# A third of the down projection's ring with its stationary chunks at other distances, modulo 512 bytes, from the moving half

## The reference

```python
up = causal_dwconv(jnp.einsum('bsd,df->bsf', h, ffn_w_up[l]), ffn_conv_w[l]) + ffn_conv_b[l]
gate, val = jnp.split(up, 2, axis=-1)
ff = jnp.einsum('bsf,fd->bsd', jax.nn.silu(gate) * val, ffn_w_down[l])
x = x + rms_norm(ff, norm_ffn_post[l])
```

## Time and profile before

| | us |
|---|---|
| median of 3 runs | 950.27 |
| lowest and highest run | 950.18, 951.21 |
| the profiled execution's span | 948.2 |
| TensorE busy | 938.9 (99%) |
| weight loads busy | 777.9 (82%) |
| DVE, ACT, POOL busy | 654.7, 433.5, 189.4 |
| down projection, first to last matmul | 732.9 to 942.6 |

### The profile page before, as it was taken

One profiled execution on the slowest core, in us unless ns is written; L12 is line 12 of the kernel. 1 busy time (PEld: TensorE's weight loads), 2 busy tenths in 40 slices (PEclk: granted clock), 3 DMA queues, 4 the chain that ended last, 5 costly groups with the idle time before them and its releaser, 6 DMA issues.

```text
span 948.2 us, 11487 instructions
## 1 busy us (share of the span) xinstructions
PE 938.9 (99%) x4419; PEld 777.9 (82%) x4419; DVE 654.7 (69%) x710; ACT 433.5 (46%) x648; POOL 189.4 (20%) x182
## 2 busy tenths in 40 slices
PE   8999999999999999999999999999999999999997
PEld 7988887887888888888888888888888888888886
DVE  6645795766655899777877787778776653535668
ACT  5524444444433555445443444444444454335353
POOL 3301000000111424242223333443431100000021
PEclk9999999999999999999999999999999999999999
DMA  6999971005322236486343446554647775677455
GB/s 225 269 328 231 209 145 45 23 23 178 134 89 89 90 97 206 142 184 183 115 141 100 145 112 133 112 143 105 140 91 208 201 235 214 228 267 264 163 171 200
DMA packets 114248, 151.16 MB, mean 159 GB/s; under 512 B 6289, under 2 KB 66193, under 8 KB 114193
## 3 DMA queue, kind: packets, MB, share of 16 engines
q1 hardware_dynamic: 100737, 118.63, 38.5%
q0 software_dynamic: 13456, 31.79, 16.8%
HBM read 113.17 MB, written 60.29 MB: 183 GB/s over the span
## 4 chain that ended last, share of the span: by engine, by line
PE 97%; DVE 1%; DMA 0%; ACT 0%; POOL 0%; issue 0%; DVEq 0%; POOLq 0%; SPq 0%; ACTq 0%
PE ps L1616 30%; PE ps L1618 30%; PE ps L1617 30%; PE ps L1626 1%; PE ps L1751 1%; PE ps L1774 1%; PE ps L1752 1%; PE ps L1760 1%; PE ps L1778 1%; DMA xin<-in_x 0%; DVE hlo L1138 0%; PE ps L1789 0%; DVE ps L1155 0%; PE ps L1664 0%; DVE x2b L1427 0%
## 5 line engine op out<-in xcount | busy, mean ns | idle before, releaser
L1616 PE MATMUL ps<-hhi,whi 128*128 128x512 f32 (+1 forms) x240 | 91.1, 379 | 0.5 <-DVE hlo L1138 0.5
L1618 PE MATMUL ps<-hhi,wlo 128*128 128x512 f32 (+1 forms) x240 | 88.5, 369 | 0.0
L1617 PE MATMUL ps<-hlo,whi 128*128 128x512 f32 (+1 forms) x240 | 88.5, 369 | 0.0
L686 POOL TENSOR_TENSOR w_sums<-wraw 128x1024 f32<-128x1024 f32 x20 | 48.4, 2421 | 185.8 <-DVE w2lo L1373 63.0
L648 POOL TENSOR_SCALAR meansq<-sumsq 128x1 f32<-128x1 f32 x28 | 10.0, 357 | 373.4 <-ACT yg L1042 170.8
L1616 PEld LDWEIGHTS ps<-hhi,whi 128*128 128x128 f32 x240 | 45.3, 189 | 8.0 <-DVE hlo L1138 0.7
L1001 ACT ACTIVATE yg<-ps,par_b 128x1024 f32<-128x1024 f32 x21 | 25.3, 1207 | 57.9 <-DVE ps L1499 57.9
L1618 PEld LDWEIGHTS ps<-hhi,wlo 128*128 128x128 f32 x240 | 45.2, 189 | 7.7
L1617 PEld LDWEIGHTS ps<-hlo,whi 128*128 128x128 f32 x240 | 45.3, 189 | 7.4 <-issue 0.5
L1447 DVE SCALAR_TENSOR_TENSOR yg<-ps,par_a,yg 128x1023 f32<-128x1023 f32 x22 | 28.2, 1282 | 26.9 <-ACT yg L1001 26.9
L1616 PE MATMUL ps<-h2hi,whi 128*128 128x512 f32 x116 | 45.4, 391 | 0.2 <-DVE wraw L1148 0.2
(11 more groups left out here) (261 smaller groups left out, 2709.1 us busy)
## 6 DMA issues: line engine op xcount, KB each, us to landing
wraw<-in_ffn_w_up SPq DMA_DIRECT2D x42, 512.0 KB, 5.2
s_dram<-in_ffn_w_down POOLq DMA_DIRECT2D x6, 2816.0 KB, 28.1
wraw<-r_dram SPq DMA_DIRECT2D x44, 256.0 KB, 3.7
wraw<-s_dram SPq DMA_DIRECT2D x44, 256.0 KB, 4.9
r_dram<-cst SPq DMA_DIRECT2D x33, 256.0 KB, 2.8
wraw<-act_dram SPq DMA_DIRECT2D x33, 256.0 KB, 3.6
wraw<-in_ffn_w_down SPq DMA_DIRECT2D x33, 256.0 KB, 4.6
wraw<-in_w_in SPq DMA_DIRECT2D x14, 512.0 KB, 10.2
```

What stands on the lines that cost most here:

```text
L686: pool.tensor_tensor(w_sums[:, 0:2, :], raw[:, 0:4:3, :], raw[:, 2:3, :].broadcast_to([P, 2, HALF]), ALU.add)\
L1616: pe.matmul(acc, w_hi, x_hi, start=first, stop=False, skip_group_check=looped)
L1617: pe.matmul(acc, w_hi, x_lo, start=False, stop=False, skip_group_check=looped)
L1618: return pe.matmul(acc, w_lo, x_hi, start=False, stop=last, skip_group_check=looped)
```

## The change

Places 4 and 5 of the ring, in dhi and dlo, get a layout of their own. They now have `SPREAD` = 1152 elements each in place of 1024. The weights lie at elements 640 to 1151. The four token chunks of 128 elements lie `CHUNK` = 144 elements apart, from element 0 in place 4 and from element 64 in place 5. So the distance from the start of a chunk to the start of the moving half is 2560 - 576 t bytes in place 4 and 2304 - 576 t bytes in place 5, where it was 2048 - 512 t bytes. Places 0 to 3 keep theirs. ACT and DVE write the activation half of places 4 and 5 with gaps, so in all products they use two instructions for these places in place of one. The order of the steps and all waits stay.

```diff
+CHUNK = P + 16
+SPREAD = 5 * P + HALF
...
-        dhi = alloc(x3_, "dhi", [P, 2, DM], F32R)
-        dlo = alloc(x3_, "dlo", [P, 2, DM], F32R)
+        dhi = alloc(x3_, "dhi", [P, 2, SPREAD], F32R)
+        dlo = alloc(x3_, "dlo", [P, 2, SPREAD], F32R)
...
-            return (((w2lo if lo else w2hi), (wlo if lo else whi), (dlo if lo else dhi))[at // 2])[:, at % 2, :]
+            return (((w2lo if lo else w2hi), (wlo if lo else whi))[at // 2])[:, at % 2, :]
+
+        def step_act(s, lo):
+            at = s % DOWN_RING
+            if at < 4:
+                return step_place(s, lo)[:, 0:HALF].rearrange("p (t c) -> p t c", t=4)
+            first = (at - 4) * (P // 2)
+            chunks = (dlo if lo else dhi)[:, at - 4, first:first + 4 * CHUNK]
+            return chunks.rearrange("p (t c) -> p t c", c=CHUNK)[:, :, 0:P]
+
+        def step_w(s, lo):
+            if s % DOWN_RING < 4:
+                return step_place(s, lo)[:, HALF:]
+            return (dlo if lo else dhi)[:, s % DOWN_RING - 4, 5 * P:]
...
-                if i == NEGATED:
-                    act.activation(hi[:, 0:HALF], raw[:, 0:HALF], ACT.Copy, scale=-1.0)
-                    act.activation(hi[:, HALF:], raw[:, HALF:], ACT.Copy).then_inc(d_rounded, 1)
+                if i == NEGATED or s % DOWN_RING >= 4:
+                    act.activation(step_act(s, False), raw_act(s), ACT.Copy,
+                                   scale=-1.0 if i == NEGATED else 1.0)
+                    act.activation(step_w(s, False), raw[:, HALF:], ACT.Copy).then_inc(d_rounded, 1)
...
+                if s // HK == NEGATED or s % DOWN_RING >= 4:
...
+                    else:
+                        dve.tensor_tensor(step_act(s, True), raw_act(s), step_act(s, False),
+                                          ALU.subtract)
+                    dve.tensor_tensor(step_w(s, True), raw[:, HALF:], step_w(s, False),
+                                      ALU.subtract).then_inc(d_split, 1)
...
-                            hi, lo = step_place(s, False), step_place(s, True)
-                            last = product(ps[:, bank + t, :], hi[:, tok], lo[:, tok], hi[:, HALF:],
-                                           lo[:, HALF:], fresh and k == 0, k == HK - 1, True)
+                            hi, lo = step_act(s, False)[:, t, :], step_act(s, True)[:, t, :]
+                            last = product(ps[:, bank + t, :], hi, lo, step_w(s, False),
+                                           step_w(s, True), fresh and k == 0, k == HK - 1, True)
```

More of the change, by code:

```diff
@@ L410, in step_place, with raw_act @@
             at = s % DOWN_RING
-            return (((w2lo if lo else w2hi), (wlo if lo else whi), (dlo if lo else dhi))[at // 2])[:, at % 2, :]
+            return (((w2lo if lo else w2hi), (wlo if lo else whi))[at // 2])[:, at % 2, :]
[10 more added lines that the diff above has]
+            return (dlo if lo else dhi)[:, s % DOWN_RING - 4, 5 * P:]
+        def raw_act(s):
+            return wraw[:, step_raw(s), 0:HALF].rearrange("p (t c) -> p t c", t=4)
         def step_raw(s):
@@ L1025, in round_step @@
                 act.wait_ge(down_landed[step_raw(s)], 32 * (s // RAW + 1))
-                hi, raw = step_place(s, False), wraw[:, step_raw(s), :]
-                if i == NEGATED:
-                    act.activation(hi[:, 0:HALF], raw[:, 0:HALF], ACT.Copy, scale=-1.0)
-                    act.activation(hi[:, HALF:], raw[:, HALF:], ACT.Copy).then_inc(d_rounded, 1)
+                raw = wraw[:, step_raw(s), :]
+                if i == NEGATED or s % DOWN_RING >= 4:
+                    act.activation(step_act(s, False), raw_act(s), ACT.Copy,
+                                   scale=-1.0 if i == NEGATED else 1.0)
+                    act.activation(step_w(s, False), raw[:, HALF:], ACT.Copy).then_inc(d_rounded, 1)
                 else:
-                    act.activation(hi, raw, ACT.Copy).then_inc(d_rounded, 1)
+                    act.activation(step_place(s, False), raw, ACT.Copy).then_inc(d_rounded, 1)
             def copy_product(i, t):
@@ L1453, in low_step @@
                 dve.wait_ge(d_rounded, s + 1)
[L1454 to L1459, removed]
-                else:
-                    dve.tensor_tensor(lo, raw, hi, ALU.subtract).then_inc(d_split, 1)
+                raw = wraw[:, step_raw(s), :]
+                if s // HK == NEGATED or s % DOWN_RING >= 4:
+                    if s // HK == NEGATED:
+                        dve.scalar_tensor_tensor(step_act(s, True), raw_act(s), -1.0,
+                                                 step_act(s, False), ALU.mult, ALU.subtract)
+                    else:
[3 more added lines that the diff above has]
+                                      ALU.subtract).then_inc(d_split, 1)
+                else:
+                    dve.tensor_tensor(step_place(s, True), raw, step_place(s, False),
+                                      ALU.subtract).then_inc(d_split, 1)
             def gate_taps(p):
@@ L1948, in _ @@
                     for t in range(4):
-                        tok = slice(t * P, (t + 1) * P)
                         if ks[0] == 0:
```

## The result

The change makes the kernel slower by 0.18%: 952.10 us (median of 16 runs, 951.83 to 952.95) against 950.34 us (16 runs, 950.10 to 951.21); the ratio is 1.0018, with a 95% interval of 1.0011 to 1.0026. The forecast was 950.5 us and the range ended at 951.5.

What follows compares the result with a forecast made beforehand. TensorE was taken as the bound: 948.2 + 0 (distances) + 0.21 (split at the end) = 948.4 us for the profiled execution, or 950.5 us as median with the same 2.07 us difference; range 948.0 to 951.5 us.

Steps and rivals of the forecast that it cites:

- The reading of before: Whole kernel: TensorE busy 939 of 948 us, so only matmul length or a gap between matmuls could move the time much.
- Step 1: Down projection, 261 moved matmuls of places 4 and 5: other distances cost zero, between 3.5 us gained and 2.8 us lost.
- The upper bound: Moved matmuls of places 4 and 5: weight load twice as long, 10.6 ns more each, 2.8 us over 261.
- Rival B: Weight loads in places 4 and 5: other distances make them longer, up to 2.8 us, 953.3 us; chance 0.10.
- Rival A: Matmuls of places 4 and 5: distance 0 makes the fixed 13.3 ns; without it 947.3 us; chance 0.13.
- The estimate from the Trainium skill's 215.7 ns: Moved matmuls: 11.0 ns of each avoidable if the distance were the reason, time near 947.9 us.
- Steps 2 and 3: Split ACT and DVE instructions in places 4 and 5: hidden except on DVE's last chain before step 76, +0.21 us.
- Rival C: Split instructions on DVE's last chain: 0.1 us more each for gaps, +0.3 us, 950.8 us; forecast with it 0.77.
- The sum: Profiled execution: 948.2 + 0 + 0.21 = 948.4 us; with the median's 2.07 us difference, 950.5 us.
- the 13.3 ns: Each 512-column matmul of the down projection: fixed part beside its column streaming, all that the change could hope to win.

Runs made afterwards that it cites:

- e2: As e1, but all chunks of places 4 and 5 start 64 bytes further, the moving half staying at element 640: 952.79 us, ratio 1.0025.
- e3: As e1, but the moving half starts 64 bytes further (element 656), the chunks staying at multiples of 512 bytes: 952.36 us, ratio 1.0022.
- e10: As e1, but only the moving half of dlo starts 128 bytes further: 951.02 us against 950.49, one run each.
- e5: As e1, but the chunks start at element 32 in place 4 and 64 in place 5: 952.58 us against 950.25, one run each.
- e13: Changed kernel with chunks 192 elements apart, from element 0 (place 4) and 64 (place 5), moving half at 896: 950.39 us against 950.36, ratio 1.0001.
- e4: As e1, but chunks and moving half both start 64 bytes further: 951.76 us against 950.27, ratio 1.0014.
- e1: Changed kernel, split instructions kept, but chunks 128 elements apart from element 0 in both places, moving half at 640: 950.40 us against 950.27, ratio 1.0002.
- e9: As e1, but in dlo alone chunks and moving half both start 64 bytes further: 951.78 us against 950.49, one run each.
- e14: As e1, but all chunks of places 4 and 5 start 16 bytes further, at element 4: 950.53 us, ratio 1.0002.
- e7: As e1, but the chunks start at element 48 in place 4 and 8 in place 5: 951.99 us against 950.25, one run each.

## Why the prediction was wrong

**The reading of before** held: TensorE is the bound, and nothing but a matmul's length or a gap could move the time. A gap didn't; a length did.

**Step 1, the price of a distance, failed** at its third point: "I take zero". The reason given there was that load and stream slide past each other through all remainders, so that a clash costs every matmul the same, whatever the distance. No run shows whether they slide, but the price is not the same for all distances: 0 and 256 modulo 512 are clean, 64 bytes off costs 2 to 7 ns on each matmul (e2, e3), and 128 bytes 8 ns on the single one that has it (e10). The upper bound, 10.6 ns, held in the mean (single gaps of 241 ns, 14 over, stand in e5): the excess less 0.1 us at step 76, (1.85 - 0.10)/261, is 6.7 ns for each moved matmul, with the aftermath in it (7.8 ns without the 36 matmuls at 256 bytes, which e13 shows to be free). Having no row for an operation, I let an argument choose the lower middle between the bounds, and gave the upper one a chance of 0.10. And with "nearest in kind" I chose rows that all lie at distance 0, so they said nothing on the question.

Part of the answer did stand in the trace of before. Matmuls of 512 columns are not 0.2267 us apart everywhere. Behind the scores of the attention, whose matmuls come 0.12 us apart, the first six take

```profile
83.42 0.40 PE L1616 MATMUL ps<-hhi,whi 128*128 128x512 f32 x1
...
84.81 0.39 PE L1616 MATMUL ps<-hhi,whi 128*128 128x512 f32 x1
```

1.39 us instead of 1.36, and the gaps to the ns, 234, 236, 228, 232, 231, 227, are, from the second on and to 1 ns, those by which e4's aftermath fades (236, 229, 232, 231, 227). So load and stream can be out of step at distance 0 as well, at 229 to 236 ns a matmul, and 226.7 is the price of being in step. ("In step" and "out of step" are names for the two kinds of gaps; no view shows the two reads themselves.) Such rows were the nearest to a matmul at another distance.

**Rival B** was the right mechanism in kind (another distance costs; 953.3 us at most), but its picture, a load twice as long, is not shown. The loads' durations stay at 0.19 us, and they say little, as they are 0.19 in the attention too, where loads start 0.11 us apart. The room in which a longer load was to be hidden didn't hide the price, 2 to 8 ns on a matmul. **Rival A** is out: none of the distances tried, eight in the changed kernel and more in the experiments, brought a step's mean clearly under 226.7 ns. The estimate from the Trainium skill's 215.7 ns (TensorE: Matmul & The Clock Gate, section "Wait — 56ns, not 53.3ns?") falls with it: no distance tried brings the trace's 226.7 any nearer to that figure.

**Steps 2 and 3, the split, held.** e1 is 0.13 us above before by the medians and 0.25 us by the stage, for a forecast of 0.21; the wait at step 76 is 0.37 us for 0.38. In the changed kernel itself it is only

```profile
936.02 0.19 PEld L1644 LDWEIGHTS ps<-dhi 128*128 128x128 f32 x1 [0.22 <-DVE dlo L1485]
936.06 0.46 PE L1644 MATMUL ps<-dhi 128*128 128x512 f32 x1
...
936.36 0.40 PE L1645 MATMUL ps<-dlo,dhi 128*128 128x512 f32 x1
```

0.22 us, because TensorE comes later to it by its slower steps 70 and 71 and their aftermath. Rival C, a dearer split for the gaps in the writes, is out by e13.

**The sum** with the price that was measured: 950.34 + 1.75 (matmuls) + 0.1 (step 76) = 952.2, for a median of 952.10. It shows that nothing else is needed; it is no forecast, as the 1.75 is read from the changed kernel's own trace.

## What to carry to other kernels

On this chip and for a dense stream of matmuls of this type, keep the starts of all stationary chunks and all moving operands at the same place modulo 256 bytes, as before, e1 and e13 do. It isn't enough that each stream agrees with the chunk loaded under it (e9: 231 ns), and groups of matmuls that are clean in themselves cost something at their borders (e4). Here a shift by 16 elements cost 2 to 7 ns on each matmul of the shifted tiles and more on up to ten behind it. When the trace shows one value for a quantity, ask first if the thing that is changed ever varied in it: 0.2267 us everywhere was no evidence, since the distance was 0 everywhere. And between bounds that no row tells apart, an argument from rates is no reason to leave a tenth to one of them.

## What the runs showed of the hardware

A dense stream of F32R matmuls of 512 columns with a weight load each runs at 226.7 ns a matmul in step, and at 229 to 234 ns in the mean out of step. In step: distances 0 and 256 bytes modulo 512, and 16 bytes with the chunk ahead, if no start changes from one matmul to the next by other than a multiple of 256 bytes (e9), or of 16 as in e14. Out of step: 4, 32, 64, 128 and 192 bytes with the chunk ahead, 16 and 64 with the stream ahead. After a disturbance, by a distance or by other matmuls between, one (e7) to ten or eleven matmuls (e3, e4) are longer until it is in step again, and the last of their gaps are often the same (236, 228 or 229, 232 or 233, 231). Why these distances, why the two directions differ, how what is ahead chooses between two patterns (229 and 233 ns at +64), whether e9 pays for changing addresses or for a matmul's own pair, and where the 13.3 ns that are left in step come from, stays open.
